# Decay rows of the chunk scan and the delta-rule heads spread over the partitions by transfers instead of matmuls, column decay as a bias of the exponential, and the scan's steps at fixed places

## The reference

```
proj = einsum('bld,de->ble', rmsnorm(x), w_in)          # 60 tiles of 128 columns
# scan, per chunk and head
cum  = cumsum(dt * A)
Lmat = exp(where(tril, cum[l] - cum[s], -inf))
y    = einsum((C B^T) * Lmat * dt, x) + (C h_prev) * exp(cum) + D * x
h    = h_prev * exp(cum_last) + S
# delta rule, per chunk and head
decay = exp(where(tril, Gc[i] - Gc[j], -inf))
T     = inverse(eye + strict(beta k k^T * decay))
attn  = (q k^T) * decay
```

## Time and profile before

| | |
|---|---|
| median of 3 runs | 1393.2 us (1392.41 to 1394.38) |
| the profiled execution, its own time | 1386.98 us |
| its span in the trace | 1385.2 us |
| TensorE matmul busy | 1302.9 us, 94% of the span |
| DVE, ACT, POOL busy | 52%, 40%, 31% |
| mean DMA rate | 100 GB/s |
| mean granted TensorE clock | 0.987 of full speed |

### The profile page before, as it was taken

One profiled execution on the slowest core, in us unless ns is written; L12 is line 12 of the kernel. 1 busy time (PEld: TensorE's weight loads), 2 busy tenths in 40 slices (PEclk: granted clock), 3 DMA queues, 4 the chain that ended last, 5 costly groups with the idle time before them and its releaser, 6 DMA issues.

```text
span 1385.2 us, 25241 instructions
## 1 busy us (share of the span) xinstructions
PE 1302.9 (94%) x10578; PEld 1240.6 (90%) x10578; DVE 713.5 (52%) x1025; ACT 559.1 (40%) x997; POOL 431.3 (31%) x405
## 2 busy tenths in 40 slices
PE   7999999899999999999999999999999979999993
PEld 6999998788899989898989889988889969999993
DVE  7764444555455656555564755397432362332224
ACT  6663333343435454545445354423223342222221
POOL 3030003232453434434452535573301150101003
PEclk9999999899999999999999999999999999999997
DMA  7334443111221111111211221366774324333323
GB/s 292 90 94 124 127 127 124 46 45 33 62 62 49 47 49 49 50 57 49 62 45 52 62 59 50 124 214 194 234 240 155 92 62 138 122 109 107 107 62 124
DMA packets 38816, 138.12 MB, mean 100 GB/s; under 512 B 4448, under 2 KB 5856, under 8 KB 38448
## 3 DMA queue, kind: packets, MB, share of 16 engines
q1 hardware_dynamic: 30384, 109.80, 25.8%
q10 hardware_dynamic: 8208, 26.22, 5.6%
q0 software_dynamic: 112, 0.50, 0.1%
HBM read 121.25 MB, written 15.24 MB: 99 GB/s over the span
## 4 chain that ended last, share of the span: by engine, by line
PE 69%; issue 10%; DVE 10%; POOL 4%; ACT 4%; DMA 2%; DVEq 0%; ACTq 0%; POOLq 0%; SPq 0%
PE ps L796 35%; PE ps L1123 16%; PE ps L688 12%; POOL w_lo L2061 2%; PE ps L744 2%; DVE conv_a L1693 2%; PE ps L748 2%; DMA out_s_ssd<-d_st 1%; DVE h_lo L1568 1%; ACT L1150 1%; DVE fin L2049 1%; ACT w_hi L1150 1%; DVE w_lo L1546 1%; POOL g_e L2127 1%; POOL s_l L2121 0%
## 5 line engine op out<-in xcount | busy, mean ns | idle before, releaser
L796 PE MATMUL ps<-h_hi,w_hi 128*128 128x260 f32 x1920 | 419.7, 300 | 16.6 <-DVE w_lo L1546 12.4
L796 PE MATMUL ps<-h_hi,w_lo 128*128 128x260 f32 x1920 | 388.1, 284 | 0.0
L796 PE MATMUL ps<-h_lo,w_hi 128*128 128x260 f32 x1920 | 388.0, 284 | 0.0
L1150 ACT ACTIVATE w_hi<-w_raw 128x512 fp32r<-128x512 f32 x352 | 212.9, 624 | 400.3 <-PE ps L796 194.3
L796 PEld LDWEIGHTS ps<-h_hi,w_hi 128*128 128x128 f32 x1920 | 299.2, 191 | 36.9 <-issue 31.4
L796 PEld LDWEIGHTS ps<-h_lo,w_hi 128*128 128x128 f32 x1920 | 298.1, 190 | 0.0
L796 PEld LDWEIGHTS ps<-h_hi,w_lo 128*128 128x128 f32 x1920 | 298.0, 190 | 0.0
L1546 DVE TENSOR_TENSOR w_lo<-w_raw,w_hi 128x512 fp32r<-128x512 f32 x216 | 157.2, 749 | 258.2 <-ACT w_hi L1150 257.9
L2061 POOL TENSOR_TENSOR w_lo<-w_raw,w_hi 128x512 fp32r<-128x512 f32 x136 | 180.2, 1328 | 253.0 <-ACT w_hi L1150 252.5
L1123 PE MATMUL ps<-y_hi,w_hi 128*128 128x260 f32 x640 | 129.0, 283 | 9.6 <-DVE y_lo L2033 5.6
L1123 PE MATMUL ps<-y_lo,w_hi 128*128 128x260 f32 x640 | 129.2, 283 | 0.0
(11 more groups left out here) (372 smaller groups left out, 1776.6 us busy)
## 6 DMA issues: line engine op xcount, KB each, us to landing
w_raw<-in_w_in SPq DMA_DIRECT2D x120, 512.0 KB, 3.6
w_raw<-in_w_out SPq DMA_DIRECT2D x40, 512.0 KB, 3.6
w_raw<-in_w_mem SPq DMA_DIRECT2D x16, 512.0 KB, 3.6
x_t<-in_x_t SPq DMA_DIRECT2D x8, 520.0 KB, 7.6
fin<-in_x_t SPq DMA_DIRECT2D x8, 520.0 KB, 4.5
out_y_t<-fin SPq DMA_DIRECT2D x8, 520.0 KB, 2.7
d_st<-in_st_ssd ACTq DMA_DIRECT2D x8, 512.0 KB, 4.8
out_s_ssd<-d_st ACTq DMA_DIRECT2D x8, 512.0 KB, 5.3
```

Of the source, the lines that this page charges most:

```text
L796: last = mm(out[:, hf, :], w[:, g % 2, P * (at_k % 8):P * (at_k % 8) + P], a[:, at_k, HALF * hf:HALF * hf + HALF], start=(at_k == 0 and j ...
L1150: return nc.scalar.activation(out, in_, func, **more)
```

## The change

- The cumulative sums of all heads are put side by side in one tile `rows_c`, transposed once on TensorE (`smallrows`), and written to a scratch of 128 x 128 floats in device memory. Each row of the scratch holds the 128 values of one head and chunk.
- Where TensorE made decay rows, SP's queue now issues a transfer that reads four rows (2 KB) and writes them to all 128 partitions (256 KB): 16 for the scan, 3 for each of 8 heads, 40 in all. `s_l` has four buffers and lies elsewhere. The matmuls with the identity and DVE's subtractions are gone.
- The column value is now the bias of ACT's exponential. A bias is one value for each partition, so an exponential of 128x512 becomes four of 128x128.
- The scan's pieces stand at fixed steps (`SSD_AT`), 23 steps a chunk from step 16 of tile 12 on, and have other neighbours; the multiply of the carried state by its decay goes from DVE to POOL; the applied state has its own two banks of PSUM (6 and 7).
- The rows of a head are loaded, masked and (for the first of the two) exponentiated ahead of `nss`.

```diff
-GDN_AT = [(-2, "nsq"), (-0.9, "nss"), (1.5, "rowa"), (2.6, "nmul"), (4, "rowax"), (6, "gram"), (8, "t0"), (14, "turn"), (16, "r1"), (18, "r2"), (20, "kend")]
+GDN_AT = [(-17, "row1"), (-7, "row1mask"), (-2, "nsq"), (-1, "row1exp"), (-0.9, "nss"), (2.6, "nmul"), (10, "rowq"), (24.8, "row2"), (29.5, "row2mask"), (6, "gram"), (8, "t0"), (14, "turn"), (16, "r1"), (18, "r2"), (20, "kend")]
-GDN_AT += [(30.5, "res"), (31, "rowg"), (32, "gramq"), (33, "fix"), (34, "qg"), (35, "attn"), (36, "wt")]
+GDN_AT += [(30.5, "res"), (31, "row2exp"), (32, "gramq"), (33, "fix"), (34, "qg"), (35, "attn"), (36, "wt")]
+SSD_AT = []
+for _c in range(NC):
+    _b = 16 + 23 * _c
+    SSD_AT += [(_b + d, ("ssd", _c, name)) for d, name in (
+        (0, "turn"), (0.8, "bcopy"), (1, "xdt"), (2, "xw"), (4.2, "inter"), (4, "xd"), (6, "interread"), (8.6, "stateps"), (10.4, "state"),
+        (12.8, "intraread"), (13.8, "ysq"), (14.9, "yred"), (16, "yln"), (17.2, "ynorm"), (19.6, "yturn"), (20.4, "ycopy"))]
+    for _q in range(4):
+        SSD_AT += [(_b + d + e * _q, ("ssd", _c, name, _q)) for d, e, name in ((3.4, 2.2, "score"), (6.4, 1.8, "intra"))]
+        if _c:
+            SSD_AT += [(_b + d + 1.8 * _q, ("ssd", _c, name, _q)) for d, name in ((-16, "row"), (-11, "mask"))]
+        SSD_AT.append((_b + (-9.9, -7.9, -6, -4)[_q], ("ssd", _c, "exp", _q)))
...
+    def row_of(first):
+
+        return rows_d[first:first + 4, :].rearrange("r t -> (r t)").unsqueeze(0).to_broadcast([P, 4 * P])
...
+            elif k == "ssd" and it[2] == "row":
+                i = 4 * it[1] + it[3]
...
+                if i >= 4:
+                    spe.wait_ge(*upto("s_intra", i - 3))
+                spe.dma_start(s_l[:, i % 4, :, :].rearrange("p h t -> p (h t)"), row_of(64 + 16 * it[1] + 4 * it[3])).then_inc(sem(f"s_row{i % 4}"), 16)
...
+            elif k == "gdn" and it[2] == "row2":
+                h = it[1]
+                spe.wait_ge(*upto("g_at", 6 * h + 5))
+                spe.dma_start(flat4(g_e2), row_of(32 + 4 * h)).then_inc(sem("g_row2"), 16)
...
-                    for j in range(4):
-                        h = 4 * qd + j
-                        last = one(side[3][:, P * j:P * j + P], cum[:, c, h:h + 1].to_broadcast([P, P]), ident)
-                    last.then_inc(sem("s_rows"), 1)
...
-                elif step == "rowa":
-                    pe.wait_ge(*upto("n_ln", 2 * h + 1))
-                    if h == 0:
-                        pe.wait_ge(*upto("row0", 2))
-                    for c in range(NC):
-                        last = one(quad(side[2])[:, c, :], row_a0[:, c, h:h + 1].to_broadcast([P, P]), ident)
-                    last.then_inc(sem("g_rowa"), 1)
...
+            elif k == "smallrows":
+                act.wait_ge(*upto("rows_ps", 1))
+                A(rows_r[:, :], side[3][:, 0:P], ACT.Copy).then_inc(sem("rows_r"), 1)
+                act.wait_ge(*upto("rows_r", 1))
+                act.dma_start(rows_d[:, :], rows_r[:, :]).then_inc(sem("rows_out"), 16)
...
-                    A(s_l[:, i % 2, :, :], s_l[:, i % 2, :, :], ACT.Exp).then_inc(sem("s_exp"), 1)
...
+                    for j in range(4):
+                        last = A(s_l[:, qd, j, :], s_l[:, qd, j, :], ACT.Exp, bias=s_ngc[:, c, 4 * qd + j:4 * qd + j + 1])
+                    last.then_inc(sem("s_exp"), 1)
...
-                    V.tensor_tensor(s_l[:, i % 2, :, :], quad(side[3]), along(cum[:, c, 4 * (s - 2):4 * (s - 2) + 4], P), ALU.subtract).then_inc(sem("s_sub"), 1)
...
-                    V.tensor_tensor(g_e1[:, :, :], quad(side[2]), along(g_ngc[:, :, h], P), ALU.add).then_inc(sem("g_sub1"), 1)
...
+                elif step == "interread" and c > 0:
+                    pool.wait_ge(*upto("s_inter", c))
+                    G.tensor_tensor(heads(s_state[:, :]), heads(s_state[:, :]), along(e_tot[:, c, 0:SSD_H], SSD_P), ALU.mult).then_inc(sem("s_decayed"), 1)
```

More of the change, by code:

```diff
@@ L178, in spread @@
     return out
-def spread_ssd(main, side):
-    padded = []
-    for it in side:
-        padded += [None] * (it in (("ssdend",),) or it[0] == "ssd" and it[2] == 1) + [it]
-    return [it for it in spread(main, padded) if it]
 def proj_items(first, last):
@@ L212, in timeline @@
     first[1, 15].append(("smallrow",))
+    for q in range(4):
+        first[10, 2 + 3 * q] = [("ssd", 0, "row", q)]
+        first[11, 2 + 3 * q] = [("ssd", 0, "mask", q)]
     for k in range(KT):
@@ L224, in timeline @@
     items += [("kvout",)]
-    side = [("ssd", c, s) for c in range(NC) for s in range(9)] + [("ssdend",)]
-    start = proj_items(a, b)
-    items += start[:FIRST] + spread_ssd(start[FIRST:], side)
+    early = {}
+    for at_step, item in SSD_AT:
+        early.setdefault(max(0, int(np.floor(at_step))), []).append((at_step, item))
     phases = {}
@@ L370, in build @@
     r_b = Region(8192)
+    s_ngc = at("s_ngc", [P, NC, SSD_H], F32, base[0])
     att_s = place("att_s", [P, 8, MEM_H * NC])
@@ L413, in build @@
     s_cb = r_side.place("s_cb", [P, SSD_G, P])
-    s_l = r_side.place("s_l", [P, 2, 4, P])
+    s_l = at("s_l", [P, 4, 4, P], F32, r_y.start)
     s_state = r_side.place("s_state", [P, SSD_W])
@@ L688, in one @@
             return mm(out, lhs, rhs, start=True, stop=True)
-        def ssd_intra(c, qd):
-            pe.wait_ge(*upto("s_scores", 4 * c + qd + 1))
-            if c > 0 and qd == 0:
-                pe.wait_ge(*upto("s_inter_read", c))
-            if c == 0 and qd == 0:
-                pe.wait_ge(*upto("s_x_read", 3))
-            for j in range(4):
-                h = 4 * qd + j
-                last = one(heads(ps[:, 4:6, :])[:, h, :], s_l[:, qd % 2, j, :], s_xdt[:, SSD_P * h:SSD_P * h + SSD_P])
-            last.then_inc(sem("s_intra"), 1)
-        def ssd_turn_y(c):
-            pe.wait_ge(*upto("s_y_normed", c + 1))
-            pe.wait_ge(*upto("s_state_new", c + 1))
-            if c + 1 < NC:
-                pe.wait_ge(*upto("s_bcopy", 2 * (c + 2)))
-            for i in range(8):
-                last = turn(ps[:, 6:8, :].rearrange("p b (i t) -> p (b i) t", i=4)[:, i, :], s_y[:, c % 2, P * i:P * i + P], ident)
-            last.then_inc(sem("s_y_turned"), 1)
         for it in items:
@@ L768, in _ @@
                 last.then_inc(sem("small_done"), 1)
+            elif k == "smallrows":
+                pe.wait_ge(*upto("row0", 3))
+                pe.wait_ge(*upto("small_step", 1))
+                turn(side[3][:, 0:P], rows_c[:, :], ident).then_inc(sem("rows_ps"), 1)
             elif k == "smallcum":
@@ L800, in _ @@
             elif k == "ssd":
-                c, s = it[1], it[2]
-                if s == 0:
+                c, step = it[1], it[2]
+                if step == "turn":
                     if c == 0:
@@ L845, in _ @@
                     last.then_inc(sem("s_stateps"), 1)
-            elif k == "ssdend":
-                ssd_turn_y(NC - 1)
+                elif step == "yturn":
+                    pe.wait_ge(*upto("s_y_normed", c + 1))
+                    pe.wait_ge(*upto("s_state_new", c + 1))
+                    for i in range(8):
+                        last = turn(ps[:, 6:8, :].rearrange("p b (i t) -> p (b i) t", i=4)[:, i, :], s_y[:, c % 2, P * i:P * i + P], ident)
+                    last.then_inc(sem("s_y_turned"), 1)
             elif k == "gdn":
@@ L919, in _ @@
                     last.then_inc(sem("g_res_ps"), 1)
-                elif step == "rowg":
-                    pe.wait_ge(*upto("g_tfi", h + 1))
-                    for c in range(NC):
-                        last = one(quad(side[2])[:, c, :], row_q0[:, c, h:h + 1].to_broadcast([P, P]), ident)
-                    last.then_inc(sem("g_rowg"), 1)
                 elif step == "gramq":
@@ L1364, in _ @@
                     A(g_pf, g_pf, ACT.Exp, scale=-0.5).then_inc(sem("n_r"), 1)
-                elif step == "rowax":
+                elif step == "row1exp":
                     act.wait_ge(*upto("g_sel1", h + 1))
-                    A(g_e1[:, :, :], g_e1[:, :, :], ACT.Exp).then_inc(sem("g_exp1"), 1)
+                    for c in range(NC):
+                        last = A(g_e1[:, c, :], g_e1[:, c, :], ACT.Exp, bias=g_ngc[:, c, h:h + 1])
+                    last.then_inc(sem("g_exp1"), 1)
                 elif step[0] == "tat":
@@ L1374, in _ @@
                         A(g_tt6, quad(side[3]), ACT.Copy).then_inc(sem("g_tt6"), 1)
-                elif step == "rowg":
-                    act.wait_ge(*upto("g_sub2", h + 1))
-                    if h:
-                        act.wait_ge(*upto("g_o_ps", 4 * h))
-                    A(g_qg[:, :, :], quad(side[2]), ACT.Exp).then_inc(sem("g_qrow"), 1)
+                elif step == "row2exp":
+                    act.wait_ge(sem("g_rowq"), 16 * (h + 1))
+                    A(g_qg[:, :, :], g_qg[:, :, :], ACT.Exp).then_inc(sem("g_qrow"), 1)
                     act.wait_ge(*upto("g_sel2", h + 1))
-                    A(g_e2[:, :, :], g_e2[:, :, :], ACT.Exp).then_inc(sem("g_exp2"), 1)
```

(3 more changed lines are left out.)

215 lines of the change are left out of this document (116 added, 99 removed).

## The result

The changed kernel takes 1328.93 us (median of 4 runs, 1327.05 to 1329.53) where the kernel before takes 1392.81 beside it (1386.75 to 1394.38). The ratio is 0.9547, 95% interval 0.9516 to 0.9577: 63.9 us faster. The forecast was 1344, range 1332 to 1362, so the direction is right and the gain is larger than the range allows.

The account below looks back on a forecast made before the run. TensorE was taken as the bound: scan 33.3 plus heads 15.7 minus 0.2 new work gives 48.8 us, so 1386.98 profiled becomes 1338.2 and the median 1393.2 becomes 1344 us, range 1332 to 1362.

Parts of the forecast that it names:

- the step that moved: Scan: one projection step fewer before `nss`, 95 instead of 96; 0.7 us not counted as gain.
- the 16 row groups: Row matmuls removed from TensorE: 13.0 us in the scan and 13.0 us in the heads.
- the walk: Scan: step-by-step count of a chunk, 26 us each; 103.4 us before any wait, plus 6 us of loss.
- start of the scan: New once: a transpose, small copies and one store, costing 0.2 us.
- Heads, removed: Heads: 16 row groups, 13.0 us, and the 2.7 us wait for the logarithm ahead of `rowa` go: 15.7 us.
- it keeps up: Heads: chain from `nss` to `gram` shortens by 1.28 and up to 0.7 us, so the time doesn't return at `gram`.
- Rival 3: More than the sum: scan loses only 2 us, heads' other waits shrink by 8: 1332 us; chance 0.11 (1328 to 1337).
- before's offset: Whole kernel: profiled execution of before lies 6.2 us below the median, so 1338.2 profiled becomes a median of 1344.
- no slack: Scan, output's turn: chain behind the last "intra" takes 5.8 us plus hand-overs against 5.8 of projection; 0.3 a chunk lost.
- Rival 1: Scan's waits stay: output's chain takes 8.9 us instead of 5.8, clock falls; loss 20, 1358 us; chance 0.26 shared with rival 2.
- Rivals 2 and 4: 2: heads give only the second row group, 1353 us, 0.26 shared with rival 1; 4: rows land late, mostly slower, 0.08.
- all three hits of the decay on the path: Scan: GpSimd's decay lengthens a DVE score multiply by 1.8 us three times; 5.4 us less gain, not added.

Follow-up runs that it names:

- e10: Changed kernel with the scan's 16 groups of four row matmuls put back on TensorE, result unused: 1342.79 us, 0.9676 of the kernel before.
- e4: Changed kernel with the heads' 16 groups of four row matmuls put back on TensorE, result unused: 1342.82 us, 0.9664 of the kernel before.
- e7: e4 with the first row's exponentials, and so the table load, behind `nss` again, without subtraction: 1345.59 us, 0.9696 of the kernel before.
- e9: e4 with both the first row's DVE subtraction and the table load behind `nss` put back: 1350.18 us, 0.9732 of the kernel before.
- e15: e9 with the second row's subtraction on DVE too, result unused: 1351.21 us, 0.9717 of the kernel before.
- e2: Kernel before with only the heads changed, the scan keeping its old order, row matmuls and subtractions: 1365.72 us, 0.9824 of the kernel before.
- e5: The changed kernel timed once more, unaltered, in a later set: 1329.60 us, 0.9581 of the kernel before.
- e14: Changed kernel with the state's decay on DVE again instead of GpSimd: 1331.01 us, 0.9579 of the kernel before.

## Why the prediction was wrong

| step of the prediction | forecast | measured |
|---|---|---|
| scan, gain, less the step that moved | 33.3 | 143.4 - 108.1 - 0.7 = 34.6 |
| of it the 16 row groups | 13.0 | 13.2 (e10) |
| of it loss left in the walk, over 103.4 | 6 | 108.1 - 103.4 = 4.7 |
| heads, gain, with that step | 15.7 | 516.1 - 492.9 + 0.7 = 23.9 |
| of it the 16 row groups | 13.0 | 11.2 (e4) |
| of it waits | 2.7 | 12.7, the rest: 7.0 idle, 5.7 busy |
| start of the scan | -0.2 | -0.5 |
| profiled execution after | 1338.2 | 1329.47 |

**The step that failed is "Heads, removed": 15.7 us.** The mechanism was right, its wait term was mis-sized: 2.7 for the one wait ahead of `rowa`, where 12.7 us went. The prediction asked whether the time comes back at `gram` and answered from one head, the fourth, in which `gram` waits 0.17; the view of waits over all heads shows 2.0 us there in five heads (`g_e`), and 2.3 and 2.4 for `g_natm` and `g_t`, of which 1.7 and 1.0 went. That it named the load of 1.28 and the subtraction of 0.69 as shortening the chain, and then let them pay for nothing but "it keeps up", is the error; e7 and e9 show that the load pays 5.0 us and both together 9.5, the 2.7 for the logarithm among them. Rival 3 had this mechanism, with 8 us of heads' waits, and got a chance of 0.11; its 1328 to 1337 holds the measured time. Of the 12.7 us, 5.7 are no wait of the view but lie in busy time of TensorE, whose ends are modelled; their cause stays open. In the runs the 23.2 us of the window are made up of 11.2 (row groups, e4), 9.5 (load and first subtraction, e9), 1.1 (second subtraction, e15) and 1.4, what e15 lacks to the 516.1 of before.

**A second, smaller step: the time the sum is set against.** The gain of the trace, 57.5, is 8.7 above the forecast; the median gained 63.9. The profiled execution of before lay 5.8 below its median, that of after 0.5 above its own. Before's executions spread, and their mean granted clock with them: in the later sets 1382.72 us at 0.986 and 1384.31 at 0.989, but 1394.10 at 0.979 and 1396.16 at 0.976. Part of this is in a stretch that the change does not touch: e2's profile, at a mean of 0.981, has

```profile
864.50:1364.00 499.50, 465.31 (x3964) 444.39 (x3963) 216.34 (x266) 151.53 (x262) 118.37 (x93) 0.96 0.43 140
```

behind the heads, 4 us more than the 495.3 above. The forecast carried before's offset over to the changed kernel as if it were the kernel's, and it took the offset from a median of three: the 38 executions of before in the later sets that took under 1400 us have a median of 1388.85, 1.9 above the profiled one. The miss of 15.1 us is thus 8.7 of the sum (1338.2 against 1329.47), 5.8 of this offset, and 0.5 by which the profiled execution after lay above its median. The smaller gain of e5's set, 59.0, still leaves its median of 1329.60 below the range that begins at 1332.

**The scan was right** in size and by its steps. `nss` starts at 338.80 (forecast about 340), the clock is at 1.00, and TensorE waits at the turns and once, for 0.6 us, ahead of the first chunk's first "intra" (walk: 0.8), nowhere above 1 us. A chunk takes 26.3 us from transposes to transposes in the first (230.68 to 256.98, walk: 26) and 27.1 in the second. The chain behind the last "intra" takes 6.5 us, from DVE's sum at 246.40 to the turn at 252.92, against 5.8 of projection: the "no slack" of the walk, and the 8.9 of the earlier trace rows did not stay. Rival 1 falls. The 0.73 that TensorE waits at this turn matches what the chain's last multiply lost: both its inputs lie in SBUF, it ran beside a multiply of GpSimd for `w_lo`, and it took 1.97 us where the other three chunks have 1.23 (timeline of DVE and POOL):

```profile
250.50 1.28 POOL L2072 TENSOR_TENSOR w_lo<-w_raw,w_hi 128x512 fp32r<-128x512 f32 x1 [1.81 <-ACT w_hi L1168]
250.89 1.97 DVE L1783 TENSOR_TENSOR s_y<-s_y,s_red 128x1024 f32<-128x1024 f32 x1 [0.92 <-ACT s_red L1168]
```

**Rivals 2 and 4 fall.** `gram` doesn't wait (rows above), and both row groups are gained (e4). The rows land in time:

```profile
s_l<-rows_d SPq DMA_DIRECT2D x16, 256.0 KB, 3.6
g_e<-rows_d SPq DMA_DIRECT2D x16, 256.0 KB, 3.6
```

The forecast had 2.4, between the transfers of 64 and 512 KB; they take as long as the 512 KB load and are hidden anyway. The weight loads behind them cost TensorE little: its waits for `w_lo` are 1.6 us in the heads (before 1.2).

**The exponentials.** Four with a bias take 1.28 us (525.65 above), where 1.1 was forecast; hidden, as was said. The walk's scores run longer beside GpSimd, also as said: 963 ns in the mean. The Trainium skill ("SBUF — State Buffer", Who interferes with whom) says that a DVE instruction with two SBUF inputs contends with a GpSimd instruction that reads SBUF, and that one with at most one SBUF input, outside the two-port modes, does not. The trace agrees: in the timeline of DVE and POOL in chunk 1, the multiply of x from PSUM takes its usual 1.22 beside `w_lo`, and a sum of 128x8 takes 1.24, until POOL is done at 263.49, where the same sum takes 0.17 alone. Not every such meeting costs DVE time: a score multiply with two SBUF inputs that starts at 261.68, within POOL's row of two instructions, takes 0.68.

```profile
260.55 1.22 DVE L1745 TENSOR_TENSOR s_xw<-ps,w_end 128x1024 f32<-128x1024 f32 x1
...
262.28 1.24 DVE L1720 TENSOR_TENSOR conv_a<-conv_a,hist 128x8 f32<-128x8 f32 x1
...
281.96 0.17 DVE L1720 TENSOR_TENSOR conv_a<-conv_a,hist 128x8 f32<-128x8 f32 x1
```

```profile
260.00 3.49 POOL L2072 TENSOR_TENSOR w_lo<-w_raw,w_hi 128x512 fp32r<-128x512 f32 x2 [3.76 <-ACT w_hi L1168]
```

By that rule with all three hits of the decay on the path the sum would have been 5.4 smaller. e14, without GpSimd's decay, is not faster, so no such loss is shown; a hit that by its numbers did lie on the path is the 0.73 above, beside `w_lo`.
